# A two-block transformer kernel on one core: first stage and S5 set-up in another order, short tables made once for all groups, some S5 copies moved to ScalarE, and float32 operands in the dilated attention

## The reference, cut to what matters

```
h = rmsnorm(x, g_pre_mix);  proj = h @ w_in          # first 512 columns: u, input of S5
lam = complex(min(a_re, -1e-4), a_im);  dt = exp(log_dt);  a_bar = exp(lam * dt)
b_bar = ((a_bar - 1) / lam) * b                      # 32 groups, 64 states, 16 channels
states = scan(a_bar, b_bar @ u);  y = Re(c @ states) + d * u
y = gelu(y);  y_a = y * sigmoid(y @ w_glu)

# dilated attention, blocks of 128 queries that see their own and the previous block of keys
s = q k^T + mask;  m = max(s);  p = exp(s - m);  den = sum(p);  o = p v / den
```

## Time and profile before

| what | value |
|---|---|
| median of 3 runs | 3806.06 us (3801.81 to 3808.69) |
| the profiled execution's own time | 3805.56 us |
| its span | 3803.7 us, 45147 instructions |
| PE busy | 3594.0 us, 94% of the span |
| DVE busy | 1584.7 us, 42% |
| POOL busy | 1055.7 us, 28% |
| ACT busy | 928.9 us, 24% |
| granted TensorE clock, mean | 0.973 of full speed |

### The profile page before, as it was taken

The page is one execution under the profiler, slowest core; times in us unless marked ns, Lnnn a source line. Parts: engine busy times, 40 slices in busy tenths (PEclk is TensorE's granted clock), DMA queues, the critical chain, the costliest instruction groups (busy, mean ns, idle before and its releaser), DMA issues.

```text
span 3803.7 us, 45147 instructions
## 1 busy us (share of the span) xinstructions
PE 3594.0 (94%) x17595; PEld 2984.3 (78%) x17595; DVE 1584.7 (42%) x2619; ACT 928.9 (24%) x1503; POOL 1055.7 (28%) x464
## 2 busy tenths in 40 slices
PE   7798999999998999999989999989799999999999
PEld 6587887788876888888768888878688778888887
DVE  5884535123226433333555555547312222222224
ACT  4122212322224111111233333334221131111112
POOL 1552010222322433333323333322122222322221
PEclk9899999999998999999989999979899999999999
DMA  4132000222131111111221111113221211111111
GB/s 130 44 77 73 12 29 1 83 72 66 50 110 72 56 47 53 44 55 44 78 72 45 32 45 45 51 55 104 89 66 61 89 50 45 49 51 44 55 44 55
DMA packets 187694, 222.74 MB, mean 59 GB/s; under 512 B 19136, under 2 KB 161052, under 8 KB 186796
## 3 DMA queue, kind: packets, MB, share of 16 engines
q1 hardware_dynamic: 172556, 165.70, 14.2%
q10 hardware_dynamic: 11936, 48.76, 3.5%
q0 software_dynamic: 3072, 6.49, 0.5%
HBM read 187.11 MB, written 31.65 MB: 58 GB/s over the span
## 4 chain that ended last, share of the span: by engine, by line
PE 76%; issue 10%; DVE 2%; ACT 1%; POOL 1%; ACTq 0%; DVEq 0%; POOLq 0%
PE ps L267 17%; PE ps L294 13%; PE ps L295 13%; PE ps L288 13%; PE ps L312 9%; PE ps L712 4%; PE ps L328 1%; PE ps L2316 1%; PE ps L2301 1%; PE ps L1900 1%; POOL wlo L259 1%; PE ps L1877 1%; PE ps L2284 1%; PE ps L2317 1%; PE ps L2282 1%
## 5 line engine op out<-in xcount | busy, mean ns | idle before, releaser
L259 POOL TENSOR_TENSOR wlo<-raw,whi 128x2048 fp32r<-128x2048 f32 (+1 forms) x162 | 699.2, 4316 | 1882.9 <-ACT whi L251 1882.1
L294 PE MATMUL ps<-h_lo,whi 128*128 128x512 f32 x1984 | 773.9, 390 | 1.4 <-POOL wlo L259 1.4
L295 PE MATMUL ps<-h_hi,wlo 128*128 128x512 f32 x1984 | 773.1, 390 | 0.0
L251 ACT ACTIVATE whi<-raw 128x2048 fp32r<-128x2048 f32 (+1 forms) x162 | 288.5, 1781 | 1098.8 <-PE ps L288 646.1
L288 PE MATMUL ps<-h_hi,whi 128*128 128x512 f32 x1984 | 499.0, 394 | 27.4 <-ACT fr L927 13.9
L288 PEld LDWEIGHTS ps<-h_hi,whi 128*128 128x128 f32 x1984 | 376.6, 190 | 108.3 <-issue 17.7
L294 PEld LDWEIGHTS ps<-h_lo,whi 128*128 128x128 f32 x1984 | 373.9, 188 | 80.4 <-POOL wlo L259 2.6
L295 PEld LDWEIGHTS ps<-h_hi,wlo 128*128 128x128 f32 x1984 | 373.6, 188 | 77.6
L1036 DVE TENSOR_TENSOR big<-big,ps 128x512 f32<-128x512 f32 x432 | 296.2, 687 | 253.0 <-PE ps L267 252.8
L267 PE MATMUL ps<-whi,f_hi 128*128 128x512 f32 x864 | 337.7, 391 | 6.5 <-DVE big L1036 6.5
L267 PE MATMUL ps<-whi,f_lo 128*128 128x512 f32 x864 | 337.5, 391 | 0.0
(11 more groups left out here) (327 smaller groups left out, 5320.4 us busy)
## 6 DMA issues: line engine op xcount, KB each, us to landing
raw<-in_w_in_dram SPq DMA_DIRECT2D x32, 1024.0 KB, 5.4
raw<-in_w_ff_dram SPq DMA_DIRECT2D x32, 1024.0 KB, 5.3
raw<-in_w_in_dram SPq DMA_DIRECT2D x49, 512.0 KB, 4.3
raw<-in_w_ffn_gate_dram SPq DMA_DIRECT2D x11, 1024.0 KB, 5.4
raw<-in_w_ffn_up_dram SPq DMA_DIRECT2D x11, 1024.0 KB, 5.3
raw<-in_w_ffn_down_dram SPq DMA_DIRECT2D x11, 1024.0 KB, 4.8
yt<-y_keep ACTq DMA_DIRECT2D x20, 512.0 KB, 4.3
raw<-in_w_out_dram SPq DMA_DIRECT2D x8, 1024.0 KB, 5.0
```

The costliest lines, as they stand in the source:

```text
L251: nc.scalar.activation(whi[c % 2][:, 0:cols], raw[c % 2][:, 0:cols], ACT.Copy).then_inc(s_hi.sem, 1)
L259: nc.gpsimd.tensor_tensor(wlo[c % 2][:, 0:cols], raw[c % 2][:, 0:cols], whi[c % 2][:, 0:cols].bitcast(F32), ALU.subtract).then_inc(s_lo.se ...
L294: nc.tensor.matmul(ps[:, bank + n, :], w(0, k, m * P, P), src[1][:, k, sl], start=False, stop=False)
L295: last = nc.tensor.matmul(ps[:, bank + n, :], w(1, k, m * P, P), src[0][:, k, sl], start=False, stop=k == ks - 1)
```

## The change

- `Start`: the four loads of `natA` and that of `log_dt` go from SP's queue to POOL's; PE no longer waits for the load of `DD` before it turns `natA`. DVE takes the turned `natA` after row tile 3 instead of 1. ACT rounds the first weight unit after row tile 5 instead of 3, the second after 7 instead of 5. SP issues the second unit's load when the first has landed.
- `S5AndConv`, PE: all eight first-half turnings come ahead of the u products, and the second-half turnings are interleaved with the first eight of them (before: the first-half ones with the first eight, the second-half ones with the next eight). In round 0, `turn_w` stands after half tile 3 instead of 7, and `inputs` after half tile 4; three half tiles lie between `inputs` and `kernel_rows`.
- `S5AndConv`, DVE: `weights(0)` comes ahead of the tables. The first 16 entries of the tables are made once for all 32 groups (`first_tables`, into `CT0`, `SN0`), and each round copies its 8 groups and makes the doublings to 32 and 64. C1, C2 and the copy of the kernel rows are made by ACT. `by_c` and `taps` stand ahead of `states`.
- Decay: the rounding and the rest of the next attention's first weight unit (`split_hi`, `split_lo` of `decay.u + 1`) move from the start of the Decay stage into the end of S5AndConv, ahead of `turned_y(3)`.
- `Dilated`: probabilities and values are single float32 tiles `PT2` and `V2`. `turned_low` and `v_low` are gone, PE waits for ACT's copy (`p_taken`, `v_taken`), a pair has one matmul of 64 columns, and DVE copies the rows instead of adding two halves.

```diff
@@ Start @@
                     if t == 3:
-                        split_hi(e, unit_no(0))
                         e.wait_ge(dv.sem, self.d + 1)
                     if t == 5:
+                        split_hi(e, unit_no(0))
+                    if t == 7:
                         split_hi(e, unit_no(1))
...
             def pool(self, e):
+                for k, name in enumerate(("s5_a_re", "s5_a_im")):
+                    for half in range(2):
+                        e.dma_start(natA[0:NG, k, half * ST:(half + 1) * ST], A[name][0]).then_inc(m["s5_ld"], 16)
+                e.dma_start(sm[:, 19, :], A["s5_log_dt"][0:1, :].partition_broadcast(P)).then_inc(m["s5_ld"], 16)
...
-                e.wait_ge(m["s5_ld"], 16 * 6)
+                e.wait_ge(m["s5_ld"], 16 * 5)
...
-                    if t == 1:
+                    if t == 3:
                         e.wait_ge(m["s5_natT"], 1)
@@ S5AndConv @@
                     load_unit(e, unit_no(self.u + j), w_cols(w, 0, O_U + 256 * j, KT, 256), (KT, 256))
+                    if j == 0:
+                        e.wait_ge(ld[0].sem, 16)
...
+                def first_tables():
+
+                    link(nc.vector.memset(CT0[:, :, 0:1], 1.0))
+                    link(nc.vector.memset(SN0[:, :, 0:1], 0.0))
+                    for j in range(4):
+                        w = 1 << j
+                        s = tm[:, 0:NG * w].rearrange("p (g k) -> p g k", g=NG)
+                        bc = lambda x: x[:, j, :].unsqueeze(2).to_broadcast([P, NG, w])
+                        cmul(CT0[:, :, w:2 * w], SN0[:, :, w:2 * w], CT0[:, :, 0:w], SN0[:, :, 0:w], bc(MR), bc(MI), s)
...
-                    link(nc.vector.memset(CT[:, :, 0:1], 1.0))
-                    link(nc.vector.memset(SN[:, :, 0:1], 0.0))
-                    for j in range(6):
+                    link(nc.vector.tensor_copy(CT[:, :, 0:16], CT0[:, gr, :]))
+                    link(nc.vector.tensor_copy(SN[:, :, 0:16], SN0[:, gr, :]))
+                    for j in (4, 5):
...
-                turn_tables(0)
                 for f in range(4):
                     weights(f)
+                    if f == 0:
+                        first_tables()
+                        turn_tables(f)
                     powers(f)
...
                     if f:
                         by_c(f, 0)
-                    states(f)
-                    if f:
                         by_c(f, 1)
                     taps(f)
+                    states(f)
                     by_b(f, 0)
...
-                for k in range(KT + 2):
-                    if k < KT:
-                        r.turn(e, 0, k)
-                    if k == 2:
-                        lo_w(0)
-                    if k >= 2:
-                        e.wait_ge(lo_made.sem, r.lo + k - 1)
-                        u_passes(0, 0, k - 2, 0)
+                for k in range(KT):
+                    r.turn(e, 0, k)
+                lo_w(0)
+                for k in range(KT):
+                    r.turn(e, 1, k)
+                    e.wait_ge(lo_made.sem, r.lo + k + 1)
+                    u_passes(0, 0, k, 0)
                 lo_w(1)
                 for k in range(KT):
-                    r.turn(e, 1, k)
                     u_passes(1, 0, k, 2)
...
                 gelu(3)
+                split_hi(e, unit_no(self.decay.u + 1))
                 turned_y(3)
@@ Dilated @@
                 def value(i, b):
-
-                    e.wait_ge(p_lo.sem, self.pl + 8 * i + b + 1)
+                    e.wait_ge(p_taken.sem, self.pt + 8 * i + b + 1)
...
                     for h in range(2):
-                        o = ps[:, 7, h * P:(h + 1) * P]
                         for c in cs:
-                            v = V2[:, i % 2, b - 1 + c, h, :, :].rearrange("p a n -> p (a n)")
-                            last = nc.tensor.matmul(o, PTH[:, b % 2, h, c, :], v, start=c == cs[0], stop=False)
-                            last = nc.tensor.matmul(o[:, 0:HD], PTL[:, b % 2, h, c, :], v[:, 0:HD], start=False, stop=c == 1)
+                            last = nc.tensor.matmul(ps[:, 7, h * HD:(h + 1) * HD], PT2[:, b % 2, h, c, :],
+                                                    V2[:, i % 2, b - 1 + c, h, :], start=c == cs[0], stop=c == 1)
```

More of the change, by code:

```diff
@@ L1219, in gate_of, with c_rows, kernel_rows @@
                                          ACT.Sigmoid).then_inc(m["s5_sg"], 1)
+                def c_rows(f):
+                    e.wait_ge(m["s5_cT"], f + 1)
+                    c_t = lambda k: ps[:, 2, k * P:(k + 1) * P].rearrange("p (g h) -> p g h", h=GRP)
+                    if f:
+                        e.wait_ge(m["s5_m2"], f)
+                    nc.scalar.activation(C1[:, :, :], c_t(0), ACT.Copy, scale=c_nsgn)
+                    nc.scalar.activation(C2[:, :, :], c_t(1), ACT.Copy, scale=-1.0).then_inc(m["s5_c"], 1)
+                def kernel_rows(f):
+                    kp = PP[0:GRP].rearrange("p a g n -> p (a g n)")[:, 0:GB * 240].rearrange("p (g n) -> p g n", g=GB)
+                    e.wait_ge(m["s5_k"], f + 1)
+                    nc.scalar.activation(kp[:, :, 7 * GRP:240], ps[0:GRP, 4:6, :].rearrange("p b (g n) -> p (b g) n", n=P),
+                                         ACT.Copy).then_inc(m["s5_kc"], 1)
                 def weights(f):
@@ L1681, in pe @@
                 for f in range(4):
-                    early = 8 if f == 0 else 3
                     half_tile(f, 0)
@@ L1690, in pe @@
                     turn_c(f)
-                    for j in range(2, early):
-                        half_tile(f, j)
+                    half_tile(f, 2)
+                    if f == 0:
+                        half_tile(f, 3)
                     turn_w(f)
-                    if f:
-                        half_tile(f, 3)
-                        early = 4
+                    half_tile(f, 3 if f else 4)
                     inputs(f)
+                    if f == 0:
+                        for j in range(5, 8):
+                            half_tile(f, j)
                     kernel_rows(f)
-                    for j in range(early, 12):
+                    for j in range(4 if f else 8, 12):
                         half_tile(f, j)
@@ L2188, in top @@
                                             AX, ALU.max, negate=True).then_inc(maxima.sem, 1)
-                def turned_low(i, b):
-                    c = self.chunks(i, b)[0]
-                    e.wait_ge(p_hi.sem, self.ph + 8 * i + b + 1)
-                    nc.vector.tensor_tensor(PTL[:, b % 2, :, c:2, :], self.turned_p(c),
-                                            PTH[:, b % 2, :, c:2, :].bitcast(F32), ALU.subtract).then_inc(p_lo.sem, 1)
                 def rows(i, b):
@@ L2208, in dve @@
                     rotate_end(0, n)
-                v_low(0, 0)
-                v_low(0, 1)
                 top(0, 0)
@@ L2218, in dve @@
                             rotate(i + 1, 1)
-                        turned_low(i, b)
                         top(i, b + 2)
@@ L2225, in dve @@
                         rows(i, b)
-                        turned_low(i, b + 1)
                         if q % 2 == 0 and more:
@@ L2232, in dve @@
                         top(i, b + 3)
-                        if q < 2 and more:
-                            v_low(i + 1, q)
                         if q == 1 and more:
@@ L2617, in _ @@
             sp.dma_start(bf[0:HEADS, :], A["fox_b_f"][0].rearrange("(h a) -> h a", a=1)).then_inc(d_vec.sem, 16)
-            for k, name in enumerate(("s5_a_re", "s5_a_im")):
-                for half in range(2):
-                    sp.dma_start(natA[0:NG, k, half * ST:(half + 1) * ST], A[name][0]).then_inc(m["s5_ld"], 16)
-            sp.dma_start(sm[:, 19, :], A["s5_log_dt"][0:1, :].partition_broadcast(P)).then_inc(m["s5_ld"], 16)
             sp.dma_start(DD[:, :], A["s5_d"][0].rearrange("g h -> h g"),
-                         allow_slow_non_contiguous=True).then_inc(m["s5_ld"], 16)
+                         allow_slow_non_contiguous=True).then_inc(m["s5_d"], 16)
             for s in stages:
```

84 lines of the change are left out of this document (37 added, 47 removed), and 2 rows, old and new, of the table m.

## The result

| | before | after |
|---|---|---|
| median | 3803.93 us (3799.12 to 3808.69, 4 runs) | 3764.73 us (3762.86 to 3768.31, 4 runs) |
| span of the profiled execution | 3803.7 us | 3760.4 us |
| PE busy | 94% | 95% |
| DVE busy | 42% | 40% |

The ratio is 0.9898, 95% interval 0.9881 to 0.9915: the change wins 39 us, and 43 us between the two profiled spans. The forecast was 3734 us, its range 3712 to 3760. The direction was right; the size was not, and the time lies just outside the range.

A forecast was written before the change was run, and what follows sets the result against it. PE, at 94% of the span, was taken as the bound. Terms 15.0 + 14.3 + 6 + 23.8 + 7 + 6 = 72.1 us off 3805.56 us gave 3733.5, stated as 3734 us; range 3712 to 3760.

The forecast's parts named there:

- the value matmuls, 23.8 us of the sum: Dilated attention outside the last pass: float32 value matmuls at 0.105 us each make 44 blocks of each kind 23.8 us shorter.
- the first rival's case: Dilated attention: the float32 matmuls win nothing, 3758 us, or cost a third more, 3775 us; chance 0.07.
- if the value matmuls lie over 0.2 us apart: Dilated attention: a stated sign that the prediction is wrong; it expected value matmuls 0.1 us apart.
- 17 us of loss as the alternative: Dilated attention value matmuls: by the four-pass rule a pair streams a third more columns, losing about 17 us.
- Forecast 7 + 6 = 13 us: Dilated attention: 7 us from ten waits for `v_low`, about 6 us from shorter last-pass loops.
- u products 0.9 us earlier: First stage: the u products start 0.9 us earlier than 28.45; bounds 3 us earlier and 2 us later.
- the "after 31" of the signs: First stage: a stated sign that the prediction is wrong, the u products starting after 31 us.
- Set-up start 42.7: Head of the S5 chain: DVE's set-up starts at about 42.7 us instead of 58.66.
- set-up 16.0 us earlier: Head of the S5 chain: DVE's set-up, its work unchanged, ends at 82.8 us, 16.0 us earlier.
- Round 0, +1.0 us: S5 round 0: DVE's chain lengthens by 1.0 us, `taps` winning nothing; `outputs` starts 15.0 us earlier, bounds 10 and 19.
- Rounds 1 to 3, 14.3 us: S5 rounds 1 to 3: PE becomes the bound, 159.5 us become 145.2, 14.3 us less; bounds 9 and 15.5.
- End of S5, 6 us: End of S5: moving the rounding earlier removes a 5.0 us wait, 6 us less; no later wait appears; bounds 4 and 8.

The follow-up runs named there:

- float32r kernel: Changed kernel with the dilated attention's value rows and turned probabilities stored as float32r, low parts left out: 3735.13 us against 3809.16 for the kernel before.
- doubled kernel: Changed kernel with every value matmul of the dilated attention issued twice: 3832.18 us against 3805.67 for the kernel before.
- second profile of the changed kernel: The changed kernel run and profiled once more, nothing altered: 3770.66 us against 3808.92 for the kernel before.
- first stage alone: Kernel before with only the first stage's reordering (loads on POOL's queue, turnings ahead of the u products, roundings two tokens later): 3793.5 us against 3808.92.
- tables by round: Changed kernel with the first entries of the turn tables made per round again, eight groups at a time: 3774.93 us against 3809.16 for the kernel before.
- memsets on POOL: Changed kernel with the two memsets of the extra rows of QA and KA moved from DVE to POOL: 3756.14 us against 3805.67 for the kernel before.
- dilated change alone: Kernel before with only the change of the dilated attention (float32 values and turned probabilities): 3789.76 us against 3805.67.
- all but the dilated attention: Kernel before with the whole change except its dilated attention part: 3781.29 us, ratio 0.9934.

## Why the prediction was wrong

**What failed: the value matmuls, 23.8 us of the sum.** The step was the count: "eight of line 1900 take 457.29 to 458.13, 0.105 us each. So four cost 0.42 us and two 0.21 us." The eight are records, and four matmuls. By the same rows a block of two chunks is 8 x 0.105 = 0.84 us (measured 0.81 to 0.83), one of one chunk 0.42 (0.39), and the term is nothing or a small loss. PE's work in the first eleven passes went from 533.4 to 531.1 us. That is the first rival's case, to which I gave 0.07, at 3758 us; the result lies 7 us above that. Of the signs of being wrong, "if the value matmuls lie over 0.2 us apart" has come true: 0.21 us a matmul, 0.24 when more are added. Rows 13 had the count, x576, and multiplying out the loops would have given 288; the argument against the rival (the transposes of `turn_p` are float32 too) compared one kind of record with another, since the transposes are single. The float32r kernel shows the cause: with one record for a matmul instead of two the block falls from 0.81 to 0.36 us; the doubled kernel shows it from the other side.

The Trainium skill says in "FP8 and Floating Point Precision", section "TensorE Precision Notes", that true float32 takes four passes. By that I had a third more passes and 17 us of loss as the alternative. The trace shows neither a third more nor half: two records as long as a float32r record (medians 275 ns), and the block of two chunks unchanged at 0.81 us. The sentence "The trace agrees with four passes for the new form" rested on the same misreading, the time of a record taken for that of a matmul. What the trace agrees with is the direction, float32 at twice the price of float32r.

**Dilated attention, waits: right, a little more than forecast.** Forecast 7 + 6 = 13 us, measured 14.4: 10.1 up to the first mask of the last pass and 4.3 in the last pass, so the two terms were off in opposite ways. PE's waits in the stage fell from 24.4 to 11.7 us. The ten waits for `v_low` are gone; a loop of the last pass went from 7.05 to 6.12 us (2493.86 to 2499.98), 4 x 0.93 = 3.7 us of the 6, and the wait of up to 3 us at the passes' end is now one for `rows`.

**u products 0.9 us earlier: wrong, 2.0 us later** (30.43), at the bound of 2; in the second profile of the changed kernel 31.46, over it and over the "after 31" of the signs. I looked for ACT's roundings as the cause, and the run with these moved refuted it. POOL's low part stops DVE's row scaling for 1.7 us in the middle of the chain; that the start would move by as much without it was not tested, and the rest of the 2.9 us is open.

**Set-up start 42.7: 46.20; set-up 16.0 us earlier: 12.6.** 2.9 us of this come from the start of the u products, the rest from steps of 1.97 us instead of 1.89. The first stage alone carried its whole 12.5 us to the first score; the mechanism was right.

**Round 0, +1.0 us: mis-sized, +2.5.** From the end of the set-up to the end of the kernel rows DVE took 35.8 us before (35.9 with the first stage alone), and takes 37.5 in the changed kernel and 34.5 with tables by round. So the tables cost 3.0 us, where I had 2.7, and the other edits won 1.4, where I had 1.7. The rest is a term that I had put at nothing, "In this round that wins nothing" of `taps`: from the end of the kernel rows to outputs(0) were 10.8 us, and are 11.6. DVE in the changed kernel:

```profile
123.45 5.63 DVE L1546 TENSOR_TENSOR_SCAN zz<-sm,zz 128x128 f32<-128x128 f32 x8
129.11 0.75 DVE L1567 TENSOR_SCALAR cacc<-vbuf,vecs 128x1024 f32<-128x1024 f32 x1
129.90 2.60 DVE L1570 SCALAR_TENSOR_TENSOR cacc<-vbuf,vecs,cacc 128x1024 f32<-128x1024 f32 x2
132.47 0.07 DVE L1552 MEMSET PP<- 128x16 f32 x1
```

The last load of `TZ` landed at 131.5, and `states` could start only at 132.5, behind `taps` and a scan that POOL had stretched from 0.42 to 2.44 us. The step that adds the diagonal is stretched in both kernels (2.42 and 2.45 us). outputs(0) is 10.1 us earlier, the very edge of the bounds of 10 and 19, and 8.7 in the second profile.

**Rounds 1 to 3, 14.3 us: 17.2 us.** 47.5 us each with PE busy throughout; I had left 48.4. Start to end of S5 27.3 us are won, where 29.3 were forecast.

**End of S5, 6 us: wrong, 1.3 us lost.** The wait for `whi` did go. "Late next is nothing" was the failed step: I asked who needs the next rounding, not what DVE owed PE. DVE's chain of softplus, scan and memsets used to end, with the first Q tile taken, just when PE came to the K products; with PE 5 us sooner it ends too late. The run with the rounding put back shows that the move wins nothing, the memsets on POOL that this chain was the bound: from last outputs to first score are 90.0 us before, 91.3 in the changed kernel and 82.9 there, 7.1 less, so the 6 us are to be had once the chain is out of the way.

**2.9 us between first score and dilated attention** are in no term. 2.6 of them lie at the end of the second attention, 16.1 us from last score to last turning before and 13.5 after. The waits there are the same (3.9 us in four, 0.5 in one), while the granted clock is lower in the kernel before than in that with the dilated change alone:

```profile
660.00:670.00 10.00, 7.44 (x34) 6.75 (x32) 4.33 (x7) 0.00 (x0) 0.00 (x0) 0.56 0.01 2
```

```profile
660.00:670.00 10.00, 6.89 (x41) 6.11 (x40) 4.25 (x7) 0.00 (x0) 0.00 (x0) 0.83 0.13 55
```

In all fourteen traces it goes with the type of the dilated operands: the four kernels with float32r there (before, all but the dilated attention, first stage alone, values as float32r) have 12.6 to 13.0 us from last score to the first of the last turnings, the ten with float32 have 10.5 or 10.6. That stage runs 1300 us later, and no run shows how its operands could bear on the clock here; the mechanism is open.

**Sum:** 10.1 + 17.2 - 1.3 + 2.9 + 14.4 = 43.3 us, the difference of the spans. 28.8 us lack to the 72.1: 23.8 are the matmuls, 7.3 the end of S5, 4.9 set-up and round 0; 2.9 in the rounds, 1.4 in the dilated waits and the 2.9 between first score and dilated attention came back. These 7.2 us were not forecast: by luck the miss is 29 us and not 36.

## What to carry to other kernels

Before pricing an instruction by a row, multiply out the loops and compare with the row's count: a float32 matmul leaves two records, and the distance between records is then half its price. Where a wait is taken away, ask every engine that PE waits for next whether it will be ready that much sooner, not only the one whose wait went. And a duration of DVE or POOL read beside an active partner holds only with that partner: idle time of the one is what the other's speed rests on, so it is not slack.

## What the runs showed of the hardware

DVE operations that stand until POOL's is done: the row scaling ends 0.55 us behind POOL's in two kernels (0.76 us alone), the long scan takes 6.63 us beside POOL and 2.28 alone and ends 2.1 behind it, and of the eight small scans, 0.42 us each alone, three took 2.04 to 2.46 us, each ending 0.3 us behind a POOL operation (9.31 us in all against 3.63). Even POOL's memset, which reads nothing, held a one-input DVE operation (0.68 us became 3.14, ending 0.5 us behind it). Where two-input operations follow one another on both sides, each waits for the other's: POOL's go from 1.04 to some 2.1 us, DVE's from 1.36 to 2.08 us, and these end 1.2 us behind POOL's.

The Trainium skill says in "SBUF — State Buffer", section "SBUF: two separate sides", that the two engines share one pair of ports as an exclusive lock, held for the whole instruction by whichever starts first, and names the DVE operations that need it: those in a two-port mode, and those with two SBUF inputs when POOL's reads SBUF. The traces agree with the lock: each of the DVE operations that waited ends behind POOL's by no more than the time that it takes alone. Which mode the one-input operations ran in, no trace here shows.

A float32 matmul with 128 stationary columns leaves two records and two weight loads, a float32r matmul or a float32 transpose one; records in a row start 0.11 us apart at full clock, with 64 or 128 moving columns.
